# Norms inside a transformer layer with a changed last step, the output turned beside the last norm, and four column blocks begun at once

## What is computed

```
x += 0.5 * g1(c) * SwiGLU_1(RMSNorm(x) * (1 + s1(c)) + b1(c))
h  = RMSNorm(x) * (1 + s2(c)) + b2(c)
[xb | yb | q | k | v] = h @ w_in
lru = RG-LRU(conv4(xb)) * gelu(yb)
att = sliding-window GQA with sinks(rope(q), rope(k), v)
x += g2(c) * ([lru | att] @ w_out)
x += 0.5 * g3(c) * SwiGLU_2(RMSNorm(x) * (1 + s3(c)) + b3(c))
final RMSNorm
```

## Time and profile before

| | us |
|---|---|
| median of 3 runs | 2426.57 (2425.94 to 2428.49) |
| the profiled execution | 2425.36 |
| its span | 2423.5 |

### The profile page before, as it was taken

One profiled execution on the slowest core, in us unless ns is written; L12 is line 12 of the kernel. 1 busy time (PEld: TensorE's weight loads), 2 busy tenths in 40 slices (PEclk: granted clock), 3 DMA queues, 4 the chain that ended last, 5 costly groups with the idle time before them and its releaser, 6 DMA issues.

```text
span 2423.5 us, 45806 instructions
## 1 busy us (share of the span) xinstructions
PE 2365.3 (98%) x17250; PEld 2260.2 (93%) x17250; DVE 1204.4 (50%) x2072; ACT 878.7 (36%) x1175; POOL 167.2 (7%) x195
## 2 busy tenths in 40 slices
PE   7999999999999999998999997999999999999998
PEld 3888999999999999997999897999999999999997
DVE  3565434434443554357667645454454454455444
ACT  3232222222223232234566534333433433433234
POOL 3000000000000000032121212000000000000002
PEclk9999999999999999999999998999999999999999
DMA  9999999888988948853453453554554554554552
GB/s 318 358 331 349 270 285 271 268 260 273 275 256 256 286 138 264 259 162 113 129 152 110 130 147 98 148 156 142 144 161 139 150 156 139 158 153 140 154 150 87
DMA packets 688437, 480.89 MB, mean 198 GB/s; under 512 B 15349, under 2 KB 611977, under 8 KB 687993
## 3 DMA queue, kind: packets, MB, share of 16 engines
q1 hardware_dynamic: 686416, 473.36, 65.3%
q0 software_dynamic: 1776, 6.26, 0.8%
q10 hardware_dynamic: 162, 0.14, 0.0%
HBM read 476.53 MB, written 5.13 MB: 199 GB/s over the span
## 4 chain that ended last, share of the span: by engine, by line
PE 91%; DVE 4%; ACT 2%; issue 1%; DMA 1%; POOL 0%; DVEq 0%; SPq 0%; POOLq 0%; ACTq 0%
PE ps L519 28%; PE ps L521 28%; PE ps L520 28%; PE ps L530 6%; PE ps L505 1%; DVE lo L1237 1%; DMA mod_raw<-in_ada_w 1%; DVE h_lo L1283 1%; DVE work L1272 0%; ACT hi L917 0%; DVE work L1524 0%; PE ps L565 0%; DVE work L1570 0%; DVE work L1526 0%; ACT work L1142 0%
## 5 line engine op out<-in xcount | busy, mean ns | idle before, releaser
L519 PE MATMUL ps<-h_hi,hi 128*128 128x320 f32 x3456 | 1081.8, 313 | 20.9 <-DVE h_lo L1283 14.5
L521 PE MATMUL ps<-h_hi,lo 128*128 128x320 f32 x3456 | 1071.6, 310 | 0.0
L520 PE MATMUL ps<-h_lo,hi 128*128 128x320 f32 x3456 | 1071.5, 310 | 0.0
L1237 DVE TENSOR_TENSOR lo<-raw,hi 128x1024 fp32r<-128x1024 f32 (+1 forms) x608 | 730.5, 1220 | 508.7 <-ACT hi L917 506.1
L917 ACT ACTIVATE hi<-raw 128x1024 fp32r<-128x1024 f32 (+1 forms) x608 | 624.4, 1050 | 936.6 <-PE ps L521 819.5
L519 PEld LDWEIGHTS ps<-h_hi,hi 128*128 128x128 f32 x3456 | 652.1, 189 | 40.8 <-issue 30.3
L520 PEld LDWEIGHTS ps<-h_lo,hi 128*128 128x128 f32 x3456 | 652.4, 189 | 0.7
L521 PEld LDWEIGHTS ps<-h_hi,lo 128*128 128x128 f32 x3456 | 652.1, 189 | 0.0
L519 PE MATMUL ps<-a_hi,hi 128*128 128x320 f32 x1376 | 426.8, 310 | 1.3 <-DVE a_lo L1391 1.3
L521 PE MATMUL ps<-a_hi,lo 128*128 128x320 f32 x1376 | 425.2, 309 | 0.0
L520 PE MATMUL ps<-a_lo,hi 128*128 128x320 f32 x1376 | 425.1, 309 | 0.0
(11 more groups left out here) (206 smaller groups left out, 913.0 us busy)
## 6 DMA issues: line engine op xcount, KB each, us to landing
raw<-in_ffn_w_gate SPq DMA_DIRECT2D x172, 512.0 KB, 4.1
raw<-in_ffn_w_up SPq DMA_DIRECT2D x172, 512.0 KB, 5.1
raw<-in_ffn_w_down SPq DMA_DIRECT2D x160, 512.0 KB, 4.7
mod_raw<-in_ada_w SPq DMA_DIRECT2D x144, 512.0 KB, 8.1
work<-in_ada_w SPq DMA_DIRECT2D x144, 512.0 KB, 8.1
raw<-in_w_in SPq DMA_DIRECT2D x56, 512.0 KB, 3.7
raw<-in_w_out SPq DMA_DIRECT2D x32, 512.0 KB, 3.8
raw<-in_ffn_w_down SPq DMA_DIRECT2D x16, 384.0 KB, 3.0
```

Source lines behind the costliest of these rows:

```text
L519: mm(out, w_hi, r_hi, start=first, stop=False)
L520: mm(out, w_hi, r_lo, start=False, stop=False)
L521: return mm(out, w_lo, r_hi, start=False, stop=last)
L1237: v.tensor_tensor(lo_slot(u)[:, 0:n], raw_slot(u)[:, 0:n], hi_slot(u)[:, 0:n], ALU.subtract).then_inc(lo_done, 1)
```

## The change

Five things are changed.

1. **Norms 1 and 2, the sum.** GpSimd adds 15 of 16 squares. PE sums this partial sum, and then the last square by a second product into the same bank.
2. **Norms 1 and 2, the root.** ACT takes Sqrt instead of Ln and Exp, and DVE the reciprocal of 128x320.
3. **Norms 1 and 2, the operand.** DVE does the low part of block k - 2 ahead of the normalised block k. Two of the samples' three steps move from GpSimd to DVE; the first (x times scale) stays on GpSimd, between the sums.
4. **The first units of the mixer and of the second feed-forward** hold four input blocks by two column blocks, instead of eight by one. PE does four column blocks at once, in four banks (`four_blocks`), with eight units. Their copies and updates come behind the seventh and eighth unit. The loops of the second feed-forward begin one step later. The sums over the sinks move behind these units.
5. **The end.** ACT multiplies x by the final weights in place, block by block. PE turns x without the factor rstd, the first 12 pieces of 48 ahead of the sums; sums and roots are by token, on the partitions (`token_sums`), and the factor is applied when the turned blocks are copied, by ACT and DVE in turn, 512 columns at a time from seven banks. Each copy has a store of its own.

```diff
             def sum_of_squares(n):
...
+                    pe.wait_ge(summed, SUMMED[n] + KB - 1)
+                    mm(psum[:, B_NORM, 0:T], ones, sum_sq, start=True, stop=False)
+                    pe.wait_ge(squared, n * KB + KB)
+                    mm(psum[:, B_NORM, 0:T], ones, sq[:, (KB - 1) % 2, :], start=False, stop=True).then_inc(ms_ready, 1)
...
+            def four_blocks(u, out, h0, half_done=None):
+
+                def step(w, q, j, m):
+                    k = q * Q + j
+                    return products(out[w][m], u + 2 * q + w, j, 2 * P, m * P, h_hi[:, k, :], h_lo[:, k, :], k == 0, k == KB - 1)
+
+                for w in range(2):
+                    arrive(u + w, None)
+                for j in range(Q):
+                    pe.wait_ge(h_ready, h0 + j + 1)
+                    for w in range(2):
+                        for m in range(2):
+                            last = step(w, 0, j, m)
+                        if j == Q - 1:
+                            last.then_inc(unit_done, 1)
+                for q in range(1, QUARTERS):
+                    for w in range(2):
+                        arrive(u + 2 * q + w, None)
...
+            def token_sums(src, b):
+                for t in range(3):
+                    rows = P if t < 2 else SAMP
+                    last = mm(psum[0:rows, b, t:t + 1], src[:, t * P:t * P + rows], ones[:, 0:1],
+                              start=True, stop=True)
+                last.then_inc(tok_ms, 1)
+
+            turn_y(0)
+            pe.wait_ge(summed, SUMMED[3] + KB - 1)
+            token_sums(sum_sq, B_NORM)
+            pe.wait_ge(squared, 3 * KB + KB)
+            token_sums(sq[:, (KB - 1) % 2, :], B_LAST)
+            for q in range(1, 4):
+                turn_y(q)
...
             def rms(n):
 
-                run(warm, eps, ACT.Ln)
+                run(warm, eps, ACT.Sqrt)
                 act.wait_ge(ms_ready, n + 1)
-                chain(run(ln_ms, psum[:, B_NORM, 0:T], ACT.Ln, bias=eps, scale=1.0 / D))
-                run(rstd, ln_ms, ACT.Exp, scale=-0.5).then_inc(rstd_ready, 1)
+                run(rms_t, psum[:, B_NORM, 0:T], ACT.Sqrt, bias=eps, scale=1.0 / D).then_inc(rms_ready, 1)
...
                         square(n, norm, x_done, x0 + CHUNKS * KB + n + 1)
+                        if norm == 3:
+                            run(x[:, n, :], x[:, n, :], ACT.Copy, scale=final_norm[:, n:n + 1]).then_inc(xg_ready, 1)
...
+            def reciprocal(n):
+                dve.wait_ge(rms_ready, n)
+                v.reciprocal(rstd, rms_t).then_inc(rstd_ready, 1)
+
             def modulate(n, sc, sh, first, end):
+                if n:
+                    reciprocal(n)
                 for k in range(first, end + 2):
+                    if n and k - 2 >= first:
+                        lo_part(n, sh, k - 2)
                     if k < end:
                         normed(n, sc, k)
-                    if k - 2 >= first:
+                        if n and k % Q == 0:
+                            samples(n, sh, k // Q)
+                    if n == 0 and k - 2 >= first:
                         lo_part(n, sh, k - 2)
...
+            for q in range(4):
+                for i, t in enumerate(Y_ORDER[q]):
+                    if Y_DONE[q, t][0] == "V":
+                        dve.wait_ge(y_turned, 3 * q + i + 1)
+                        rows = P if t < 2 else SAMP
+                        v.tensor_scalar(y_tok[0:rows, t, 4 * q * P:4 * (q + 1) * P], psum[0:rows, Y_BANK[q, t], :],
+                                        rstd_tok[0:rows, t:t + 1], None, ALU.mult).then_inc(y_copied_2, 1)
```

## The result

The changed kernel takes 2408.77 us (median of 4 runs, 2407.27 to 2410.44) against 2426.44 us of the kernel before (4 runs, 2425.94 to 2428.49). The ratio is 0.9926, with a 95% interval from 0.9911 to 0.9941: faster by 17.7 us, where 14.3 were forecast, and inside the range of 2408 to 2417, near its lower end. The profiled execution took 2407.99 us, with a span of 2405.5 against 2423.5.

The account below looks back on a forecast made before the run. PE's waits at the two norms inside the layer and the unhidden end were taken as the bound. Gains of 2.0, 4.8 and 7.5 us sum to 14.3, from 2426.57 to 2412.3 us; range 2408 to 2417.

Parts of the forecast that it names:

- The chain ahead of the mixer: Norm before the mixer: last square, sum, table load, root, reciprocal (2.1 us); first normalised block at 1107.0, against 1107.64 before.
- T: Start of the first normalised operand block behind a norm: 1107.0 before the mixer, 1477.8 before the second feed-forward.
- The relay from operand blocks to fifth unit: Behind each norm: sixteenth operand block at T+18.15; fifth unit's low part at T+21.45 before the mixer, T+22.0 before the second feed-forward.
- The gate itself: Behind each norm PE can do 96 products, then needs the fifth unit, split only after the last of 16 operand blocks.
- the rival in which the order does nothing: Low parts' order at both norms does nothing, as DVE waits for ACT's high part: 3.2 us each, 2418.7; chance 0.04.
- The 96 products: Products on the first four units behind a norm: 16.4 us without a wait, 4.9 of it at the half clock.
- The second norm: Before the second feed-forward: one unit needed instead of two, table load gone; 4.8 us gained, clock loss of 1.7 us unchanged.
- the rival of 2410.6: No clock loss behind the second norm, and none elsewhere: 1.7 us less, 2410.6; chance 0.17.
- The end: From the last product to the span's end: first copies end at 2406.65, stores end at 2416.0 against 2423.5, 7.5 us gained.
- The rival in which they keep the rate of before: At the end, stores take 11.5 us as before, not the busy engines' rate: 3.8 us later, 2416.1; chance 0.10.
- The reciprocal's rivals: Reciprocal at both norms at a bound: 0.5 us each, 2409.1, chance 0.05; 2.8 each, 2413.7, chance 0.13.
- the slower case: Reciprocal without fixed cost, scaling as a whole: from 9.3 us on slower; at 26.5 us, 2461; chance 0.03.

Follow-up runs that it names:

- e1: Changed kernel with the four-block start undone, two column blocks side by side again in mixer and second feed-forward; 2412.74 us, ratio to before 0.994.
- e3: Changed kernel with the low part of block k - 2 behind the normalised block k again; 2416.13 us, ratio to before 0.9952.
- e9: Changed kernel with all twelve final copies of 512 columns on ScalarE, six of them were on VectorE; 2410.17 us.
- e7: Changed kernel with the fifth unit split inside the operand pass, ahead of operand block 12; 2407.01 us, ratio to before 0.9914.
- e2_old_end: Changed kernel with the new end undone: last norm by features with Ln and Exp, turned and copied as before; 2415.64 us, ratio to before 0.9952.
- e5: Changed kernel with GpSimd adding all 16 squares at the two norms inside the layer, one product with ones; 2411.43 us, the only run.

## Why the prediction was right, and where its sizes were off

**The chain ahead of the mixer: right.** T was set at 1107.0 and came at 1107.08 (6.0 us behind the start of the last product, and 5.9 measured); the reciprocal at 2.1 took 2.15, between the bounds of 0.5 and 2.8. The second product in the shade of the load, the root at 0.53 (0.51), all as put. The slope between two tiny forms of the same operation was a good price for a form forty times as large. The Trainium skill's repeat count (VectorE: DVE Perf Modes, First, the fixed hardware budget), from which the estimate was 2.7 us, is not borne out as a rate per element: 2.15 us less the fixed part is 6.2 to 6.3 ns for each of 320.

**The relay from operand blocks to fifth unit: right as a mechanism, 1.4 too long.** The sixteenth block was set at T + 18.15 and came at T + 16.69 (1123.77). The mis-sized term is the samples: four times 1.0 us, where the four pairs took 0.79 to 0.80; I had taken a gap between the dependent steps and had the back-to-back price only as the lower bound. That is 0.8. The rest, 0.7, is in the blocks: 0.79 instead of 0.81 is 0.3 over fifteen, and only 14 low parts stand ahead of the sixteenth block, where I had counted 15, which is 0.4. The 0.2 at the start was there (0.17). From there to the fifth unit it was 3.38, against 3.3. So the fifth unit came 1.4 to 1.5 us earlier than forecast at each norm (T + 20.1 and T + 20.5 against 21.45 and 22.0), and this is the mixer stage's surplus: 3.6 instead of 2.0.

**The gate itself: shown.** The early split removed both waits and shortened the feed-forward stage by 1.2, and the mixer stage by 1.6 against the kernel with the same fall of the clock; without that it gave nothing there. The four-block start without it gave nothing before the mixer. The low part behind the next block moved the fifth unit by 2.3 us at both norms, so the rival in which the order does nothing is out. The forecast's price for it, 0.2 for each of 16 or 3.2, was too high: 13 blocks stand directly behind a low part, 2.7, and 0.4 of that is hidden behind ACT's split.

**The 96 products: 15.9 us, forecast 16.4.** PE ran at the half clock for 3.4 us behind its restart before the mixer, where 4.9 were carried over from the earlier trace rows. The waits for operand blocks inside this stretch, three of 0.33 to 0.44 in the kernel before, are gone as forecast.

**The second norm: 7.5 instead of 4.8.** Three sizes: the fifth unit earlier (T 0.2 and the pass 1.5, 1.8 in all), and the clock. I had counted its loss of 1.7 behind the wait as unchanged "as the new wait is as long"; the wait was 1.02 and not 2.5, and the loss is gone. This was the rival of 2410.6, with 0.17, and together with the shorter passes, at both norms, it is why the measurement lies at the range's lower end. The chance of 0.17 was put on it for shorter waits, and the wait was shorter, but that this kept the clock up isn't shown. Against these stands a new wait of 0.40 for a hidden block (L1533). From 6.6 (earlier fifth unit) and 1.7, less 0.4, it should be 7.9; 0.4 of it I can't place. The argument from the wait's length was weak in any case: behind 3.13 us in e1 the clock held, behind 2.41 in e3 it fell. So that part of the surplus is luck.

**The end: 7.1 instead of 7.5.** First copies were to start 4.8 behind the last product and did at 4.46, the copies were done 8.5 behind it and not 9.9, a copy took 0.68 on ScalarE and 0.74 on VectorE for the 0.75 assumed. The stores then took 10.2 us from first issue to end, not 9.4: a store lands 3.1 after its issue when the next one is already in the engines, not 2.4. That the stores, and not the copies, are the bound is shown by e9. The rival in which they keep the rate of before was priced wrongly in the forecast: 11.5 us from the first issue at 2406.65 end at 2418.15, which is 2.1 later than 2416.0 and not 3.8, so 2414.4 and not 2416.1. The measured 10.2 lies between the two, 0.8 above my 9.4 and 1.3 below that rival. The engines' 7.8 us of work are the same in both kernels and read from the trace; that they, and not SyncE's issuing, set the 10.2 isn't shown.

**The sum** missed by 3.4 to 3.7 us: +1.6, +2.7, -0.4, and -0.2 for the head. The reciprocal's rivals, the order that does nothing and the slower case fell by the traces. Of the parts of the change, in their own stages: the new end 7.2; the low part's order 3.8 at each norm, 1.5 of it with a fall of the clock; the lone last square 1.7 and 1.8; the four-block start 0 and 1.9 (4.0 by the medians); the samples on DVE 0.7 each; root and reciprocal against Ln and Exp -0.4 and +0.1, read at the first operand product. These can't be added: most of them shorten the same relay, and each was undone alone.

## What to carry to other kernels

Where several slow pieces of one relay stand in a fixed order on two engines, find the one that the waiting engine needs next and ask what stands ahead of it in program order; here a split that took 1.2 us stood behind four blocks' work that was not yet needed, and moving it removed waits of 1.35 and 1.02 us. The wider start alone left the gate where it was; what it did was to free the first unit early enough for that move. Price a small dependent step from a row with the same two steps, not from a rule: a block directly behind the low part that it waits for came 0.61 us after it, 0.2 more than without the wait, while the samples' add, which also waits for the step directly ahead, made a pair of 0.79 us with it, as if it did not wait. Cut a trace at the same products in both kernels and compare stage by stage: effects of 0.7 us showed there which a median of whole runs did not. But one trace is one execution: look at where the clock fell in it before two stages are compared, and at the other runs' times, which in e1_two_blocks told of 2 us that the trace did not have.

## What the runs showed of the hardware

- The granted clock falls to one half (1.2 GHz), for 3.4 us or longer, after PE has waited, and not after every wait. The same 1.74 us wait near 1350 us had the fall behind it in the changed kernel and not in e7, whose waits there were the same up to that point; 3.13 us had none, 2.41 had one. What decides it is open. A fall was free ahead of another wait (2.2 instead of 3.7 us of it), and cost 1.6 in dense work. The runs of one kernel spread by 1 to 4 us; one or two such falls would make that, which isn't shown, as one run of each has a trace. The heads, alike but for a table load near their end, differ by up to 3.2 us (1099.83 to 1102.98), nearly all of it in the first 90 us; the shortest, in e2_old_end, is the only one whose clock did not fall near 50 us.
- GpSimd's steps slow VectorE's: 0.48 us alone, 0.73 to 0.94 with GpSimd at work on tiles of 128x256.
- The product with ones has two prices, 0.81 us and 1.44. The second is its price at the half clock: in e5 and at the end of the kernel before the clock had fallen during PE's wait for it. In the changed kernel the product starts at 1470.53 at the second norm, ahead of the fall at 1475.2, and takes 0.81, where the prediction took 1.15.
- SyncE's twelve final issues take 7.0 us in the changed kernel and 7.4 in e9: 0.84 to 1.30 for a pair of 256 KB stores and 0.47 to 1.04 for one of 128 KB. In e2, where the old end leaves pauses between them, a pair takes 0.81 to 0.84 and a single one 0.47 to 0.54. Whether the issuing or the DMA engines hold them back was not tried.
